# Last job of the expert loop written out, its rows combined by a one-hot product, with one-pass gathers and a still-weight router product

## The reference

```python
logits = x @ w_router                       # 304 x 8
top_val, top_idx = lax.top_k(logits, 2)
top_w = softmax(top_val)
out = sum over e of gate[:, e] * swiglu(x, w_gu[e], w_down[e], 3584)
x = layer_norm(ALPHA * x + out, g, b)       # rows of 1024
```

## Time and profile before

| | |
|---|---|
| time, median of 3 runs | 1871.73 us (1868.35 to 1873.22) |
| the profiled execution | 1873.19 us, span 1871.6 us |
| PE, DVE, ACT busy | 1759.1, 1410.6, 1106.2 us |
| mean granted TensorE clock | 0.970 |

### The profile page before, as it was taken

The page is one execution under the profiler, slowest core; times in us unless marked ns, Lnnn a source line. Parts: engine busy times, 40 slices in busy tenths (PEclk is TensorE's granted clock), DMA queues, the critical chain, the costliest instruction groups (busy, mean ns, idle before and its releaser), DMA issues.

```text
span 1871.6 us, 27226 instructions
## 1 busy us (share of the span) xinstructions
PE 1759.1 (94%) x9561; PEld 1493.5 (80%) x9561; DVE 1410.6 (75%) x1544; ACT 1106.2 (59%) x1144; POOL 86.6 (5%) x174
## 2 busy tenths in 40 slices
PE   6999999999989998999999999899999999999990
PEld 5988999998858887958877787688888888887870
DVE  4998655457355665668988888888888888888885
ACT  4545543236344544337887777677777777777771
POOL 0000000000104440010000000000000000000001
PEclk9999999999888999979999999999999999999995
DMA  9653454443303331059999999999999999999963
GB/s 232 201 205 88 121 157 152 141 134 102 104 9 98 110 102 47 2 213 365 349 351 336 339 355 341 356 375 368 377 373 380 368 385 359 382 373 373 381 238 107
DMA packets 229128, 460.89 MB, mean 246 GB/s; under 512 B 16533, under 2 KB 121652, under 8 KB 229025
## 3 DMA queue, kind: packets, MB, share of 16 engines
q1 hardware_dynamic: 217438, 433.76, 64.8%
q10 hardware_dynamic: 6067, 18.86, 2.8%
q0 software_dynamic: 5536, 7.12, 1.4%
HBM read 441.40 MB, written 18.76 MB: 246 GB/s over the span
## 4 chain that ended last, share of the span: by engine, by line
issue 55%; PE 35%; DVE 5%; ACT 3%; DMA 1%; POOL 1%; SPq 0%; POOLq 0%; ACTq 0%; DVEq 0%
PE ps L1963 7%; PE ps L1965 6%; PE ps L1964 6%; PE ps L2335 3%; PE ps L2038 3%; PE ps L2304 2%; PE ps L2009 1%; PE ps L2330 1%; PE ps L2354 1%; PE ps L2355 1%; DMA xtok<-in_x_sample 1%; ACT x_hi L969 1%; ACT w_hi L906 0%; PE ps L2200 0%; ACT xres L968 0%
## 5 line engine op out<-in xcount | busy, mean ns | idle before, releaser
L1864 DVE TENSOR_TENSOR w_lo<-raw,w_hi 128x2048 fp32r<-128x2048 f32 x212 | 484.0, 2291 | 78.0 <-ACT w_hi L1182 78.0
L1182 ACT ACTIVATE w_hi<-raw 128x2048 fp32r<-128x2048 f32 x212 | 406.0, 1919 | 157.3 <-PE ps L2550 151.9
L1873 DVE TENSOR_TENSOR w_lo<-raw,f_hi 128x2048 fp32r<-128x2048 f32 x126 | 283.0, 2282 | 25.5 <-PE ps L2451 17.1
L1191 ACT ACTIVATE f_hi<-raw 128x2048 fp32r<-128x2048 f32 x126 | 237.8, 1914 | 72.5 <-PE ps L2451 49.0
L2548 PE MATMUL ps<-w_hi,g_hi 128*128 128x512 f32 x560 | 220.0, 393 | 3.4 <-DVE w_lo L1864 3.4
L2550 PE MATMUL ps<-w_hi,g_lo 128*128 128x512 f32 x560 | 218.2, 390 | 0.0
L2549 PE MATMUL ps<-w_lo,g_hi 128*128 128x512 f32 x560 | 218.1, 389 | 0.0
L1963 PE MATMUL ps<-x_hi,w_hi 128*128 128x304 f32 x672 | 208.9, 311 | 5.9 <-DVE w_lo L1315 3.3
L1965 PE MATMUL ps<-x_lo,w_hi 128*128 128x304 f32 x672 | 203.6, 303 | 0.0
L1964 PE MATMUL ps<-x_hi,w_lo 128*128 128x304 f32 x672 | 202.8, 302 | 0.0
L1315 DVE TENSOR_TENSOR w_lo<-raw,w_hi 128x2048 fp32r<-128x2048 f32 (+4 forms) x129 | 135.5, 1096 | 61.0 <-ACT w_hi L906 60.8
(11 more groups left out here) (435 smaller groups left out, 3158.2 us busy)
## 6 DMA issues: line engine op xcount, KB each, us to landing
raw<-in_moe_w_gu SPq DMA_DIRECT2D x224, 1024.0 KB, 6.6
raw<-in_moe_w_down SPq DMA_DIRECT2D x112, 1024.0 KB, 6.8
raw<-in_ffn_w_gu SPq DMA_DIRECT2D x44, 512.0 KB, 4.9
kvn<-in_cache_ckv SPq DMA_DIRECT2D x128, 128.0 KB, 2.4
raw<-in_conv_w_in SPq DMA_DIRECT2D x16, 512.0 KB, 8.3
raw<-in_ffn_w_down SPq DMA_DIRECT2D x16, 512.0 KB, 4.4
rows_in<-zrow ACTq DMA_DIRECT2D x13, 512.0 KB, 4.9
raw<-in_conv_w_out SPq DMA_DIRECT2D x8, 512.0 KB, 6.8
```

Source lines behind the costliest of these rows:

```text
L1182: nc.scalar.activation(w_hi[:, u % SPLIT], raw[:, u % RAW], ACT.Copy).then_inc(hi_done, 1)
L1191: nc.scalar.activation(first_hi(k), first_raw(k), ACT.Copy).then_inc(hi_done, 1)
L1864: V.tensor_tensor(w_lo[:, u % SPLIT], raw[:, u % RAW], w_hi[:, u % SPLIT].bitcast(F32), ALU.subtract).then_inc(lo_done, 1)
L1873: V.tensor_tensor(w_lo[:, (U_MOE + k) % SPLIT], first_raw(k), first_hi(k).bitcast(F32), ALU.subtract).then_inc(lo_done, 1)
```

## The change

Router: `w_rt` stands still and the 304 columns of each `xres` chunk move; the 8 x 304 logits are copied and turned into token rows by three transposes, which PE does after the first group of row transposes. ACT writes the rows twice, as `xt_hi` (fp32r) and `xt`; DVE makes `xt_lo`. The gathers are then two fp32r products (`gather_upper`, `gather_lower`) instead of one float32 product. The start of `acc`, the table of jobs, the weights and the reading of the table into registers move from ahead of the first unit into the first units (k = 4 to 8, the table after chunk 3).

Last job: the loop runs over one job less, and the last job is written out. Adding the halves of jobs H, A and B and storing them moves to POOL, in the first loop job. In the last job DVE computes which row of each token is in it (`last_places`), DVE builds a slot-by-weight one-hot `last_t`, PE turns it, POOL gathers the rows of all other jobs from DRAM (rows that lie in the last job read a place that is not used), and DVE adds them at k = 12 to 17. After the last unit PE multiplies the one-hot `comb` with `y_row`, straight from SBUF, and DVE adds that. The layer norm takes its sum, mean and squares on ACT. SP stores the result, and its two empty loads after the loop go.

```diff
-            for b, (t0, n) in enumerate(TB):
-                m = nc.tensor.matmul(ps[0:n, LOGIT_BANKS[b], 0:NEXP], xres[:, c, t0:t0 + n], w_rt[:, c],
+            m = nc.tensor.matmul(ps[0:NEXP, 2, 0:T], w_rt[:, c], xres[:, c], start=c == 0, stop=c == DC - 1)
...
+                for a, (t1, w) in enumerate(TB):
+                    m = nc.tensor.transpose(ps[0:w, 4, NEXP * a:NEXP * a + NEXP], lgT[:, t1:t1 + w], ident[0:NEXP, 0:NEXP])
...
+            nc.scalar.activation(xt_hi[0:n, b, 512 * hf:512 * hf + 512], ps[0:n, ROW_BANKS[i], :], ACT.Copy)
             nc.scalar.activation(xt[0:n, b, 512 * hf:512 * hf + 512], ps[0:n, ROW_BANKS[i], :], ACT.Copy).then_inc(rt_act, 1)
...
+        def rows_lower_part(b):
+            v.wait_ge(rt_act, 2 * b + 2)
+            V.tensor_tensor(xt_lo[0:n, b], xt[0:n, b], xt_hi[0:n, b].bitcast(F32), ALU.subtract).then_inc(rows_lo, 1)
...
-        pe.wait_ge(xpose_free, DC + 1)
-        idle(16, ROW_BANKS[0])
+        pe.wait_ge(rt_act, 1)
+        idle(20, ROW_BANKS[0])
         pe.wait_ge(rt_act, 6)
-        for c in range(2):
-            gather(c)
-        pe.wait_ge(xpose_free, DC + 6)
-        for c in range(2, 4):
-            gather(c)
-        pe.wait_ge(table_ready, 1)
+        for c in range(3):
+            gather_upper(c)
+        for c in range(3):
+            gather_lower(c)
+        gather(3)
...
+            if k == TABLE_AT:
+                v.wait_ge(table_ready, 1)
+                n_jobs = v.value_load(...)
+                last_job = v.value_load(...)
...
+        pool.wait_ge(f_fl, len(DOWN_N))
+        for x, to in halves:
+            nc.gpsimd.tensor_copy(to[0:HALF], y_p[PACKED[x]][HALF:P]).then_inc(f_fc, 1)
+        for i, (x, half) in enumerate(halves):
+            pool.wait_ge(f_fc, i + 1)
+            nc.gpsimd.tensor_tensor(y, y, half[0:HALF], ALU.add).then_inc(f_fd, 1)
...
+                if last and k == 0:
+                    last_places()
+                if last and k == 4:
+                    v.wait_ge(y_st, n_jobs * 16 + ZERO_STORES * 16)
+                    V.tensor_copy(slot_i[:, 1], rows_f).then_inc(last_dve, 1)
+                if last and k in ADD_AFTER:
+                    add_row(ADD_AFTER[k])
...
+        with pe.Fori(0, last_job) as j:
+            job(j)
+        job(last_job, True)
+        pe.wait_ge(last_act, 1)
+        pe.wait_ge(last_act, 2)
+        for b, (t0, n) in enumerate(TB):
+            for h in range(2):
+                if h == 1 and b == 0:
+                    pe.wait_ge(last_dve, 1 + 3 + 1)
+                m = nc.tensor.matmul(ps[0:n, COMB_BANKS[b] + h, :], comb[:, t0:t0 + n], y_row[:, 512 * h:512 * h + 512],
+                                     start=True, stop=True, skip_group_check=True)
+            m.then_inc(last_pe, 1)
...
+            nc.scalar.activation(sqt[0:n], acc[0:n, b], ACT.Copy, accum_out=stat[0:n, b, 0:1]).then_inc(fin_a, 1)
+            nc.scalar.activation(stat[0:n, b, 1:2], stat[0:n, b, 0:1], ACT.Copy, scale=-1.0 / D).then_inc(fin_a, 1)
+            nc.scalar.activation(sqt[0:n], acc[0:n, b], ACT.Square, bias=stat[0:n, b, 1:2], accum_out=stat[0:n, b, 2:3]).then_inc(fin_a, 1)
             nc.scalar.activation(stat[0:n, b, 3:4], stat[0:n, b, 2:3], ACT.Sqrt, scale=1.0 / D, bias=eps[0:n, 0:1]).then_inc(fin_a, 1)
```

More of the change, by code:

```diff
@@ L1781, in _ @@
         V.tensor_tensor(tk[:, 2], tk[:, 1], tk[:, 0], ALU.subtract).then_inc(rt_dve, 1)
-        for i in range(3):
-            acc_start(i)
-        v.wait_ge(rt_pe, 8)
+        rows_lower_part(0)
+        v.wait_ge(rt_pe, COUNTED)
         counts = ps[:, 4, 3 * NEXP:4 * NEXP]
@@ L1828, in _ @@
[L1828 to L1842, removed]
-        n_jobs = v.value_load(jobi[0:1, MAX_JOBS:MAX_JOBS + 1], min_val=NEXP - FIRST_JOBS, max_val=MAX_JOBS - FIRST_JOBS)
+        rows_lower_part(1)
+        rows_lower_part(2)
+        def job_table():
+            chain(V.tensor_tensor(cmp_[:], jobf[:, 0:MAX_JOBS].unsqueeze(2).broadcast_to([P, MAX_JOBS, NEXP]),
+                                  starts[:].unsqueeze(1).broadcast_to([P, MAX_JOBS, NEXP]), ALU.is_ge))
+            chain(V.reduce_sum(jobf[:, 0:MAX_JOBS], cmp_[:], AX))
+            chain(V.tensor_scalar(jobf[:, 0:MAX_JOBS], jobf[:, 0:MAX_JOBS], -1.0, None, ALU.add))
+            chain(V.reduce_sum(jobf[:, MAX_JOBS:MAX_JOBS + 1], jobs[:], AX))
+            chain(V.tensor_scalar(jobf[:, MAX_JOBS + 1:MAX_JOBS + 2], jobf[:, MAX_JOBS:MAX_JOBS + 1], -1.0, None, ALU.add))
+            V.tensor_copy(jobi[:], jobf[:]).then_inc(table_ready, 1)
@@ L1847, in rows_lower, with weights @@
+        def weights():
+            v.wait_ge(rt_act, 7)
+            chain(V.tensor_scalar(tk[:, 4], tk[:, 3], 1.0, None, ALU.add))
+            chain(V.reciprocal(tk[:, 4], tk[:, 4]))
+            chain(V.tensor_tensor(tk[:, 5], tk[:, 4], tk[:, 3], ALU.mult))
         def rows_lower(n, bank):
@@ L1933, in _ @@
                     V.tensor_tensor(hT_lo[:, to], of, hT_hi[:, to].bitcast(F32), ALU.subtract).then_inc(m_hTl, 1)
-                if k - 1 == NEXT_AFTER:
+                if k - 1 == NEXT_AFTER and not last:
                     rows_lower(j + 2, 6)
-        for i, (x, half) in enumerate(zip("HAB", (half_p, sg_p, hh_p))):
-            v.wait_ge(f_fc, i + 1)
-            y = y_p[PACKED[x]][0:HALF]
-            V.tensor_tensor(y, y, half[0:HALF], ALU.add).then_inc(f_fd, 1)
-        v.wait_ge(y_back, 6 * 16)
@@ L1950, in _, with add_last @@
-        v.wait_ge(fin_ld, 32)
-        for b, (t0, n) in enumerate(TB):
+        with v.Fori(0, last_job) as j:
+            job(j)
+        job(last_job, True)
+        v.wait_ge(unit_used, n_jobs * JOB_UNITS + (FIRST_JOBS * JOB_UNITS + U_MOE))
+        v.wait_ge(y_st, n_jobs * 16 + ZERO_STORES * 16)
+        V.tensor_copy(y_row[:, 512:D], ps[:, 5, :]).then_inc(last_dve, 1)
+        v.wait_ge(fin_ld, 32)
+        def add_last(b):
+            n = TB[b][1]
+            bank = COMB_BANKS[b]
+            v.wait_ge(last_pe, 2 + b + 1)
+            V.tensor_tensor(acc[0:n, b], acc[0:n, b], ps[0:n, bank:bank + 2, :].rearrange("p b n -> p (b n)"), ALU.add).then_inc(fin_v, 1)
@@ L2520, in _, with job @@
             k += 1
-        with pe.Fori(0, n_jobs) as j:
+        def job(j, last=False):
             for k, (kind, s, part) in enumerate(ORDER):
```

245 lines of the change are left out of this document (166 added, 79 removed).

## The result

The changed kernel takes 1851.56 us (median of 4 runs, 1850.26 to 1853.03); the kernel before took 1870.04 us beside it (4 runs, 1868.14 to 1873.22). The ratio is 0.9908, with a 95% interval of 0.9893 to 0.9922. The sign was as forecast; the gain is 18.5 us where 27 were predicted, and the time is 6.6 us above the 1845.

The account below looks back on a forecast made before the run. Loop jobs taken as PE-bound, DMA close behind (share 0.99). 9.3 + 29.4 + 0.6 - 0.6 - 4.8 - 6.6 = 27.3 us gained: profiled 1873.2 to 1845.9, against the median 1844.5, say 1845 us; range 1837 to 1852.

Parts of the forecast that it names:

- router and the chain of DVE, to unit 0: Head: logits compared 1.3 us earlier and work moved from ahead of unit 0, which starts 4.7 us earlier.
- POOL in the first loop job: First loop job: each POOL copy or add holds up one w_lo; 4.8 us lost, range 0 to 8.6.
- last job: Last loop job: 6.6 us lost to places (1.7) and adds (4.9), 0.6 us gained by fewer turned blocks.
- end: After PE's last product: 19.5 us instead of 48.9, ACT being the chain; 29.4 us gained.
- The clock gives less: Rival, head: router and gathers 4 to 7 at half clock, 4.0 + 3.4 us less gain, 1852 us; chance 0.06.
- 0.143 each, 3.4 us: Head, gathers 4 to 7: 24 fp32r products of 320 columns replace 7.99 us of float32; 4.6 us gained.
- Go into units 4 to 7, where it has gaps: First jobs: about 3 us of DVE work, acc starts and weights, fits DVE's gaps in these units.
- the rival with two passes: Rival, first loop job: POOL's two-input adds take two passes, 8.6 us lost instead of 4.8, 1848 us; chance 0.13.
- nothing, up to 3 us: Last job: cost of six gathers bringing 608 rows, 2.5 MB, 6.5 us of a nearly full queue.
- A unit's load has about 5 us to spare: Last job: slack of about 5 us in weight loads, given for the row gathers costing nothing.
- Rows late: Rival, last job: gathers land 10 us or more after k = 12, DVE and PE wait, 1855 us or more; chance 0.08.
- 15 us of room: Last job: time between the end of the six gather issues (+25.5) and DVE's first add (+40.8).

Follow-up runs that it names:

- e4: Changed kernel with the third token block of the gathers filled up from 48 to 128 rows with zeros; 1841.98 us, ratio 0.9854.
- e1: Changed kernel with POOL's three copies and three adds of the first loop job left out; 1846.61 us, ratio 0.988.
- e2: Changed kernel with POOL's three copies and three adds replaced by six fills that read nothing; 1843.59 us, ratio 0.9867.
- e9: Changed kernel with the second and third starts of acc moved to k = 14 and 15, the weights to k = 16; 1850.7 us, ratio 0.9893.
- e10: e7 with the second and third starts of acc and the weights moved to k = 14 to 16; 1828.03 us, ratio 0.9778.
- e6: Changed kernel with the last job's adds spread over k = 18 to 34 and only 16 rows per row gather; 1843.78 us, ratio 0.9861.
- e7: Changed kernel with 128-row gather blocks, POOL's six operations spaced, last job's places at k = 4, row gathers one after another, adds spaced; 1829.85 us.
- e8: The kernel before the change, unchanged, profiled once more; 1869.63 us, span 1868.0 us.

## Why the prediction was wrong

By its own steps, measured against predicted. The last column holds what is left net of the 4.3 us ahead of the router; it sums to 15.9 us (20.2 - 4.3).

| step | predicted | measured |
|---|---|---|
| router and the chain of DVE, to unit 0 | +4.7 | +4.6 |
| gathers 4 to 7, to unit 1 | +4.6 | +0.4 |
| unit 1 and the displaced work, to 1209 us | -0.6 | -2.4 |
| POOL in the first loop job | -4.8 | -6.5 |
| last job | -6.0 | -10.3 |
| end | +29.4 | +30.1 |

- **Router and unit 0: right in the sum.** The shift of the logits was 1.8 us net where 1.3 were predicted. "The clock gives less" was wrong in its first half (router at 1.00), and half right in its second: the clock fell in the middle of gathers 4 to 7, and in only three of six profiles of them.
- **"0.143 each, 3.4 us" for gathers 4 to 7: failed, and it is the largest mis-sized term.** 8.1 us were measured, 4.7 more. (The table shows 4.2 of them, since unit 0 took 6.5 us instead of the 7.1 of before.) The price came from back-to-back products of one shape, and e4 shows that it holds for those (3.5 us). It left out that every third product has 48 rows. The change of shape cost 3.0 us of the 4.7 (6.55 us with it and 3.5 without, both at full clock). The kernel before has the same 48-row products, in float32: the earlier trace rows has them in one line of 24, and only the loads of its trace show the idle 0.44 us. The other 1.6 us are the clock, which fell to 0.50 under these products here and not in e1, e2 and e9, with the same products. So the spacing alone doesn't bring it down; what does stays open.
- **"Go into units 4 to 7, where it has gaps": failed.** Around units 5 to 7 DVE runs back-to-back w_lo, in the kernel before as well. It cost 1.4 us (e10), and the clock in unit 1 another 1.0 (the lead falls from 9.27 at 826 us to 8.24 at 842), a fall that e1, e2 and e9 don't have either. The 0.6 us for the registers was not seen.
- **POOL, 4.8 us: the mechanism was right, the size too small.** 6.5 us (e1). The price was made from an iota that has no input, 1.27 us for 1024 columns. Less the w_lo that it waits for, a copy is worth about 0.9 us and an add 2.2 (estimates from the 3.1 and 4.4 us above); put into the prediction's own sum they give 2.7 + 6.6 - 1.5 - 1.3 = 6.5. So the mis-sized term is the adds, and the rival with two passes had the better price for them (2.5) beside too high a one for the copies. The Trainium skill, GPSIMD Engine Reference, section 3.1, gave 2.25 us as an estimate for an add: the record of an add is 4.4 us, and agrees once the w_lo is taken off. With 2.25 the prediction's sum comes to 7.8, not to its "about 7".
- **Last job: two terms mis-sized, one of them counted as nothing.** The places took 1.9 us (1.7 predicted) and the adds' queue up to 4.35 (4.9 predicted). The gathers' 2.5 MB, "nothing, up to 3 us", cost 4.5 (e6): 6.5 us of transfers in 25 us, beside a queue with a DMA share of 0.99, made ACT wait up to 3.5 us for a load. "A unit's load has about 5 us to spare" was the wrong part, for such a burst; one gather after another (e7) costs almost nothing. "Rows late" didn't happen, but by little: the last gather was issued from 1734.63 to 1736.7 and landed 8.8 us after it began, at 1743.4; the adds began at 1746.19 and waited for nothing. Of the "15 us of room" between the last issue and the first add 9.5 were there, since the issues took 2.0 to 3.0 us instead of 1.25, and the landing took 6.7 of them; had the first add come at the planned +40.8 (it came at +44.3), DVE would have waited 0.7 us for the rows.
- **End: right**, 30.1 against 29.4, with the order of engines as described.
- **Own time.** The sum was made against a profile that was 3.1 us late before the changed part began. That made the lead at unit 1 look right. Against e8 the span shrank by 16.6 us.

One slip: the loop job that begins at 1702.29 is the fifth and last, not the fourth; no number hung on it.

## What to carry to other kernels

Work that is moved into a saturated loop costs by how it queues, not by its sum: adds of 1.28 us one at a time cost next to nothing (e7), six in a row up to 4.35 of their 7.9 us, and the same holds for POOL's reads of SBUF and for a burst of gathers beside a full weight queue. Before pricing a product from a row, compare its shapes, and also those of its neighbours: the change of shape had the price here. And compare a landmark ahead of the change in both profiles before reading any lead behind it, and the granted clock of the stages between: here it moved the time by 1.4 to 3.0 us at two places that the edits of a run didn't touch.

## What the runs showed of the hardware

- TensorE: a change between weights of 128 and of 48 rows costs about 0.2 us each at full clock in fp32r products of 320 columns (three products 0.83 us mixed, 0.44 us at 128 rows or at 48 throughout).
- POOL's copy and add of 64 x 1024 float32 from SBUF, which alternate with w_lo, take 3.1 and 4.4 us, and stretch w_lo from 2.23 to 3.3 us from start to start, in the mean over eight. Pieces of 512 columns (1.9 and 2.6 us), one between two w_lo, cost the jobs nothing (120.58 us each). Fills of the same tiles take 0.95 us and stretch nothing.
- An indirect gather of 128 rows of 4 KB took 2.4 to 2.7 us to issue while DVE and the weight queue were busy (0.94 to 0.98 us at the end of the kernel before), and landed about 10 us after the issue began (4.3 to 7.2 at that end).
- The granted clock behind a PE wait of 2.6 us fell in some runs of nearly the same program and not in others, at a price of 1.4 to 2.7 us; likewise in the middle of the same gathers (0.50 in three profiles, 1.00 in three).
